# Rotary halves exchanged by transfers within SBUF instead of products on TensorE

## The chip, the cores and the metric

The kernel runs on one core of one Trainium2 chip. The metric is the device time of one execution in microseconds (us). The kernel before takes 1118.47 us, the median of three runs (1117.57 to 1119.99).

## The reference

Input is 256 tokens of width 1024. First comes one block with conditioning (scale, shift and gate from a vector c): a SwiGLU feed-forward, a token mixer and a second feed-forward. Then come two layers, each with retention (4 heads of 64), sliding-window attention with sinks (6 query and 2 key heads), latent attention (6 heads of 64 + 32 rotary dimensions), an output projection, a layer norm and a mixture of 16 experts. What the change touches is the rotary embedding of queries and keys: in the mixer (12 heads of 64), for retention's q and k (4 heads of 64), and for the last 32 dimensions of the latent queries and its one key.

```python
def apply_rope(t, cos, sin):
    t1, t2 = jnp.split(t, 2, axis=-1)
    return jnp.concatenate([t1 * cos - t2 * sin, t2 * cos + t1 * sin], axis=-1)
```

Written with the two halves of a head exchanged, this is t * cos + swap(t) * (-sin on the first half, +sin on the second).

## The kernel before

The kernel is written engine by engine, each with its own list of instructions in a fixed order, and semaphores between them; nothing schedules them later. Activations lie feature by token: 128 features on the partitions, 256 tokens along the row, so the two halves of a head are on different partitions. SBUF is the chip's working memory, PSUM the memory that TensorE (PE) writes.

Weights come from memory in units of up to 1 MB. SyncE (SP) issues their loads in order (`load`, L553 to L561) into a ring of six slots; a load waits until the slot's unit of six before has been read (`lo_made`). ScalarE (ACT) makes a half-precision copy `whi` (L444), VectorE (DVE) the remainder `wlo` (L469), and PE multiplies the pieces (L750). DVE does so for a unit three ahead of PE (`ahead` and `unit`), between its other tasks, in the order in which the code has them.

Mixer 1 projects the heads in six pairs of tiles (r = 0 to 5). Pair by pair: PE projects into PSUM; ACT evicts the raw projection to `qraw1` (`proj_out`); PE multiplies it by a 128x128 matrix `rot` of 0, 1 and -1 that exchanges the halves with their signs (`rot1`, L1119 to L1125, `rot_mm`); DVE does the rope in three operations (L2407: exchanged times sine, L2409: raw times cosine, L2410: the sum, `rope_out`).

Each layer has six ropes: r=0 the latent key (32 rows), r=1 and 2 retention's q and k, r=3 to 5 the latent queries in three pairs of heads, each with a rotation on PE in bank 7 (`rot2`, L1240 to L1247). Two more products on PE (L1383, L1384) exchange the two key heads of the sliding-window attention, `sk`, and ACT evicts the result (L2050, `swap_out`), for `scores(0)` on PE needs both orders. PE's order in this part is: projections of retention's q and k, UQ (latent queries), UKV, retention's v and gate, with `scores(p)`, `turn(p)` (transposes) and `values(p)` of six pairs of attention heads, and `ret_scores`, in between. `scores(3)` waits for `ret_d`, the four decayed products of DVE (`decayed`, L2667). DVE's order is: ropes, low parts, maxima (L2623), normalisation, copies of transposes (L2656), decays.

Of the kernel before, what the change touches and what calls it, by code (L numbers as in the profile page):

```python
# [85 lines left out]
C_IDENT, C_ROT, C_ROTM, C_ONES, C_INVF, C_EPS, C_EPSLN, C_PRIO16, C_PRIO4 = 0, 128, 256, 384, 512, 513, 514, 516, 532  # L86
# [10 lines left out]
def constants():  # L97
# [3 lines left out]
    for b in (0, 64):  # L101
        for i in range(32):
            small[b + 32 + i, C_ROT + b + i] = -1.0
            small[b + i, C_ROT + b + 32 + i] = 1.0
    for i in range(16):
        small[80 + i, C_ROTM + 64 + i] = -1.0
        small[64 + i, C_ROTM + 80 + i] = 1.0
# [27 lines left out]
    cosr, sinr = np.cos(ang64), np.sin(ang64)  # L135
    ang32 = (t[None, :].astype(np.float32) * np.tile(inv32, 2)[:, None]).astype(np.float32)
    cosm, sinm = np.ones((P, T), np.float32), np.zeros((P, T), np.float32)
    cosm[64:96], sinm[64:96] = np.cos(ang32), np.sin(ang32)
# [36 lines left out]
def build(nc, a, out):  # L175
    small_d, b1_d, b2_d = a["const_small"], a["const_block1"], a["const_block2"]
    with ExitStack() as ctx:
# [37 lines left out]
        rot = small[:, C_ROT:C_ROT + P]  # L215
# [42 lines left out]
        qraw1 = [rt1[:, 512 * i:512 * i + 512] for i in range(2)]  # L258
        rtmp1 = [rt1[:, 1024 + 512 * i:1536 + 512 * i] for i in range(2)]
# [30 lines left out]
        qraw2 = [rt2[:, 512 * i:512 * i + 512] for i in range(2)]  # L290
        rtmp2 = [rt2[:, 1024 + 512 * i:1536 + 512 * i] for i in range(2)]
# [74 lines left out]
        proj_out, rot_mm, rope_out = sem("proj_out"), sem("rot_mm"), sem("rope_out")  # L366
# [5 lines left out]
        swap_mm, swap_out, gn_in = sem("swap_mm"), sem("swap_out"), sem("gn_in")  # L372
# [177 lines left out]

        block = ctx.enter_context(nc.Block())
# [3 lines left out]
        def _(sp):  # L555
# [46 lines left out]
            for l in range(LAYERS):  # L602
                for i in range(N_LMIX):
                    load(Unit(U_L + N_L * l + i), sources[U_L + N_L * l + i])
                units, wholes = moe_units(l)
# [7 lines left out]
                for i, src in enumerate(units):  # L613
# [131 lines left out]
        def _(pe):  # L745
# [375 lines left out]
            def rot1(r):  # L1121
                pe.wait_ge(proj_out, 1 + r + 1)
                if r >= 2:
                    pe.wait_ge(rope_out, r - 1)
                pe.matmul(ps[:, 4 + r % 2, :], rot, qraw1[r % 2], start=True, stop=True).then_inc(rot_mm, 1)  # L1125

            proj_by_tokens([(Unit(U_MIX + IN1_POS[i]), 256, i) for i in range(3)], 0, [(x_new, 4), (gt_out, 4)], used)
            for i in range(2, 10):
# [10 lines left out]
                if 2 <= i < 8:  # L1139
                    rot1(i - 2)  # L1140
# [87 lines left out]
            for l in range(LAYERS):  # L1228
# [11 lines left out]
                def rot2(r, e, rows, mat):  # L1240
                    left(e)
                    if r == 1:
                        pe.wait_ge(swap_out, l + 1)
                    elif r:
                        pe.wait_ge(rope_out, rb + r)
                    n = T if rows.start else HALF
                    pe.matmul(ps[rows, 7, 0:n], mat, qraw2[r % 2][rows, 0:n], start=True, stop=True).then_inc(rot_mm, 1)  # L1247

                def rot_mla(j):
                    rot2(3 + j, 9 + j, slice(0, 96), small[0:96, C_ROTM:C_ROTM + 96])  # L1250

                def scores(p):

                    if p == 0:
                        pe.wait_ge(mask_made, 1)
                        pe.wait_ge(swap_out, l + 1)
# [108 lines left out]
                rot2(0, 3, slice(64, 96), small[64:96, C_ROTM + 64:C_ROTM + 96])  # L1365
# [15 lines left out]
                left(5)  # L1381
                pe.wait_ge(rope_out, rb + 1)
# [13 lines left out]
                rot2(1, 7, slice(0, P), rot)  # L1396
# [5 lines left out]
                rot2(2, 8, slice(0, P), rot)  # L1402
                turn(1)
                scores(2)
                rot_mla(0)
# [9 lines left out]
                rot_mla(1)  # L1415
# [3 lines left out]
                rot_mla(2)  # L1419
# [303 lines left out]
        def _(act):  # L1723
# [81 lines left out]
            def phase(ph):  # L1805
# [74 lines left out]
            for i in range(10):  # L1880
# [9 lines left out]
                elif i < 7:  # L1890
                    r = i - 1
                    if r >= 2:
                        act.wait_ge(rope_out, r - 1)
                    dst = qraw1[r % 2]
# [67 lines left out]
            for l in range(LAYERS):  # L1962
# [43 lines left out]
                def mla_query(j):  # L2006
# [4 lines left out]
                    act.wait_ge(rope_out, rb + 2 + j)  # L2011
                    leave(9 + j, qraw2[(3 + j) % 2][0:96, :], ps[0:96, j % 2, :])
# [20 lines left out]
                leave(3, qraw2[0][64:96, 0:T], ps[64:96, 5, 0:T])  # L2033
# [15 lines left out]
                act.wait_ge(swap_mm, l + 1)  # L2049
                act.activation(sk[:, 1, :], ps[:, 7, 0:T], ACT.Copy).then_inc(swap_out, 1)  # L2050
# [9 lines left out]
                leave(7, qraw2[1], ps[:, 0, :])  # L2060
# [4 lines left out]
                act.wait_ge(rope_out, rb + 1)  # L2065
                leave(8, qraw2[0], ps[:, 1, :])
# [914 lines left out]
```

## Time and profile before

| | |
|---|---|
| median of three runs | 1118.47 us |
| the profiled execution, time | 1117.76 us |
| the profiled execution, span | 1116.0 us |
| PE busy | 1077.0 us (97%) |
| DVE busy | 874.7 us (78%) |
| ACT busy | 633.1 us (57%) |
| granted TensorE clock | 0.99 |

The span is the time from the first to the last recorded instruction; the execution takes 1.8 us more. A start time in the views is counted from the span's start. Mixer 1's rotations lie between 244 and 279 us, those of the first layer between 589 and 640, those of the second between 861 and 913. Busy shares are averages; what a stretch waits for stands in the chain of waits and in the idle time before an instruction.

### The profile page before, as it was taken

The page shows a single profiled execution, that of the slowest core. Times are in us where ns is not written, and L with a number is a line of the kernel's source. Part 1 is how long each engine was busy: PE and PEld are TensorE (multiplying, and loading weights), DVE is VectorE, ACT ScalarE, POOL GpSimd, SP SyncE. Part 2 cuts the span into 40 slices and gives each one's busy share as a digit, 9 for nine tenths or more (in the row PEclk, how much of TensorE's full clock was granted, in tenths as well). Part 3 has the DMA queues.
Part 4 walks back from the last instruction along what each step waited for, and adds up shares of the span by engine and source line. Part 5 has one row for each costly group of instructions (what it writes and reads, how often), then busy time and mean ns, then how long its engine had stood idle before and what let it go on. Part 6 is the DMA issues. An engine that isn't in the chain of part 4 may idle for free.

```text
span 1116.0 us, 24969 instructions
## 1 busy us (share of the span) xinstructions
PE 1077.0 (97%) x10736; PEld 819.0 (73%) x10736; DVE 874.7 (78%) x1130; ACT 633.1 (57%) x792; POOL 90.5 (8%) x104
## 2 busy tenths in 40 slices
PE   6999999999999999999999999999999999999996
PEld 5677777688788577777778785877758877597773
DVE  4789699788787885554667967999966886799994
ACT  1544344463466554444367555877755755687771
POOL 1114621043000110000000000000000000000000
PEclk9899999999999999999999999999999999999998
DMA  9999799754556578554546226499993523579981
GB/s 340 370 371 373 278 316 359 247 177 160 189 187 229 195 254 305 194 184 167 175 143 237 94 77 231 184 378 416 414 315 107 183 89 108 222 263 396 416 363 39
DMA packets 134717, 271.94 MB, mean 244 GB/s; under 512 B 9428, under 2 KB 98104, under 8 KB 126296
## 3 DMA queue, kind: packets, MB, share of 16 engines
q1 hardware_dynamic: 124248, 231.79, 58.1%
q0 software_dynamic: 7904, 29.25, 7.3%
q10 hardware_dynamic: 2464, 9.44, 2.2%
q8 instruction: 77, 1.26, 0.5%
q14 instruction: 24, 0.20, 0.0%
HBM read 269.41 MB, written 1.05 MB: 242 GB/s over the span
## 4 chain that ended last, share of the span: by engine, by line
PE 81%; DVE 10%; ACT 4%; DMA 3%; issue 2%; ACTq 0%; DVEq 0%; SPq 0%
PE ps L750 67%; PE ps L1625 3%; DVE wlo L469 3%; DMA area<-in_w_ada_dram 2%; PE ps L1673 1%; PE ps L892 1%; PE ps L902 1%; DVE area L2841 1%; PE ps L910 1%; PE ps L1278 1%; PE ps L1247 1%; PE ps L1087 1%; DVE bnst L2282 1%; ACT area L1776 1%; PE ps L1308 1%
## 5 line engine op out<-in xcount | busy, mean ns | idle before, releaser
L469 DVE SCALAR_TENSOR_TENSOR wlo<-raw,whi 128x2048 f16<-128x2048 f32 (+4 forms) x212 | 466.0, 2231 | 36.6 <-ACT whi L444 36.0
L444 ACT ACTIVATE whi<-raw 128x2048 f16<-128x2048 f32 (+4 forms) x212 | 385.2, 1850 | 25.8 <-DMA raw<-in_w_ffn_in_dram 10.2
L750 PE MATMUL ps<-uhi,whi 128*128 128x256 f16 (+2 forms) x1328 | 329.6, 260 | 2.2 <-DVE ulo L2308 2.0
L750 PE MATMUL ps<-uhi,wlo 128*128 128x256 f16 (+2 forms) x1328 | 329.4, 260 | 0.0
L750 PE MATMUL ps<-ulo,whi 128*128 128x256 f16 (+2 forms) x1328 | 329.4, 260 | 0.0
L750 PE MATMUL ps<-whi,hreg 128*128 128x512 f16 (+1 forms) x656 | 205.0, 381 | 0.0
L750 PE MATMUL ps<-area,whi 128*128 128x96 f16 (+2 forms) x2168 | 155.0, 210 | 0.0
L750 PEld LDWEIGHTS ps<-area,whi 128*128 128x128 f16 (+2 forms) x2168 | 145.4, 99 | 11.7 <-issue 5.6
L750 PE MATMUL ps<-area,wlo 128*128 128x96 f16 (+2 forms) x1084 | 149.4, 210 | 0.0
L750 PEld LDWEIGHTS ps<-uhi,whi 128*128 128x128 f16 (+1 forms) x1328 | 130.3, 98 | 23.5 <-issue 8.9
L750 PEld LDWEIGHTS ps<-ulo,whi 128*128 128x128 f16 (+1 forms) x1328 | 130.2, 98 | 15.6 <-issue 1.9
L750 PEld LDWEIGHTS ps<-uhi,wlo 128*128 128x128 f16 (+1 forms) x1328 | 130.1, 98 | 11.5
L750 PE MATMUL ps<-wlo,hreg 128*128 128x512 f16 (+1 forms) x328 | 124.9, 381 | 0.0
L750 PEld LDWEIGHTS ps<-whi,hreg 128*128 128x128 f16 (+1 forms) x656 | 68.9, 105 | 70.6 <-issue 3.0
L750 PEld LDWEIGHTS ps<-area,wlo 128*128 128x128 f16 (+2 forms) x1084 | 107.3, 99 | 0.0
L2359 DVE SCALAR_TENSOR_TENSOR area<-area,cond 128x512 f32 (+1 forms) x94 | 72.0, 766 | 10.7 <-DMA area<-in_w_ada_dram 7.5
L1796 ACT ACTIVATE hreg<-ps 128x512 f32<-128x512 f32 x22 | 13.2, 599 | 117.1 <-PE ps L750 117.1
L750 PEld LDWEIGHTS ps<-wlo,hreg 128*128 128x128 f16 (+1 forms) x328 | 34.5, 105 | 33.5 <-issue 2.1
L2325 DVE SCALAR_TENSOR_TENSOR hreg<-ps,hreg 128x512 f32<-128x512 f32 x22 | 15.1, 688 | 46.2 <-ACT hreg L1796 46.2
L549 POOL DMA_DIRECT2D area<-in_w_ada_dram x48 | 35.0, 729 | 161.8 <-DVE area L2359 129.6
L1798 ACT ACTIVATE hreg<-hreg 128x512 f16<-128x512 f32 x22 | 13.9, 632 | 56.2 <-DVE hreg L2325 56.2
L750 PE MATMUL ps<-whi,uhi 128*128 128x256 f16 (+2 forms) x176 | 38.8, 244 | 2.0 <-DVE ulo L2310 2.0
(358 smaller groups left out, 1324.6 us busy)
## 6 DMA issues: line engine op xcount, KB each, us to landing
raw<-in_exp_w_gate_up_dram SPq DMA_DIRECT2D x64, 1024.0 KB, 8.4
raw<-in_w_ffn_in_dram SPq DMA_DIRECT2D x44, 1024.0 KB, 7.5
raw<-in_w_in_dram SPq DMA_DIRECT2D x34, 1024.0 KB, 7.0
area<-in_w_ada_dram POOLq DMA_DIRECT2D x48, 512.0 KB, 7.1
raw<-in_w_ffn_out_dram SPq DMA_DIRECT2D x22, 1024.0 KB, 7.6
raw<-in_exp_w_down_dram SPq DMA_DIRECT2D x22, 1024.0 KB, 9.2
raw<-in_w_out_dram SPq DMA_DIRECT2D x12, 1024.0 KB, 4.9
x<-in_exp_w_down_dram SPq DMA_DIRECT2D x6, 1024.0 KB, 10.1
```

The source lines that it names most:

```text
L444: act.activation(whi[:, u.slot, 0:n], raw[:, u.slot, 0:n], ACT.Copy, scale=SW)\
L469: dve.scalar_tensor_tensor(out=wlo[:, u.slot, 0:n], in0=raw[:, u.slot, 0:n], scalar=SW, in1=whi[:, u.slot, 0:n], op0=ALU.mult, op1=ALU.sub ...
L549: eng.dma_start(aring[:, j, :, :], w_ada[:, 2 * j:2 * j + 2, c0:c0 + ADA_BLOCK]).then_inc(ada_late[j], 16)
L750: last = pe.matmul(o, st, mv, start=start and i == 0, stop=stop and i == 2, skip_group_check=True)
L892: ins = pe.transpose(ps[:, 4 + 2 * t + k // 4, (k % 4) * P:(k % 4 + 1) * P], xn[:, t, k * P:(k + 1) * P], ident)
L902: pe.matmul(ps[:, bank, :], ident16, zeros16[:, :], start=True, stop=True)
L910: pe.matmul(o, st[:, k, xs], res_one, start=k % 4 == 0 and i == 0, stop=False, skip_group_check=True)
L1625: last = pe.matmul(ps[0:SLOTS, 6 + n, :], e_whole[i % 4][:, f * SLOTS:(f + 1) * SLOTS], whole[i % 2][:, f * D + n * HALF:f * D + (n + 1) * ...
L1796: act.activation(s_act, ps[:, 4 + 2 * par, :], ACT.Silu, scale=1.0 / S).then_inc(silu_made, 1)
L1798: act.activation(hhi[:, par, :], h_f32, ACT.Copy).then_inc(h_hi, 1)
L2325: dve.scalar_tensor_tensor(out=h_f32, in0=ps[:, 5 + 2 * par, :], scalar=SX / S, in1=s_act, op0=ALU.mult, op1=ALU.mult).then_inc(h_made, 1)
L2359: ins = dve.scalar_tensor_tensor(out=v, in0=w, scalar=cond[:, k:k + 1], in1=v, op0=ALU.mult, op1=ALU.add)
```

## The change

ACT now evicts a projection straight to the place where the rotated tile is to stand. SP issues transfers from SBUF to SBUF (`swap_halves`) that copy each half to the other half's partitions of a second tile `swp`; DVE multiplies that by the sine, the tile in place by the cosine, and adds. The signs of the rotation matrix stand in the sine tables (for the mixer by a column `sign` as the scale of ACT's sine). All rotation products and the two exchange products leave PE, and ACT no longer evicts the exchanged `sk`. The latent ropes work on the 32 rotary rows only. In the mixer a swap is four transfers of 32 rows of 2 KB; in a layer it is two transfers of 16 rows (latent key, and each pair of latent queries), two of 64 rows (`sk`) or four of 32 rows (retention): 24 in the mixer and 18 in a layer, 60 in all. Each swap waits for the landing of the swap before it.

```diff
+            def swap_halves(landed, halves, src, dst):
+                if landed > 32 * len(halves):
+                    sp.wait_ge(swap_in, landed - 32 * len(halves))
+                for a0, b0, n in halves:
+                    sp.dma_start(dst[a0:a0 + n], src[b0:b0 + n]).then_inc(swap_in, 16)
+                    sp.dma_start(dst[b0:b0 + n], src[a0:a0 + n]).then_inc(swap_in, 16)
+
             for i in range(N_MIX):
                 load(Unit(U_MIX + i), sources[U_MIX + i])
+                r = i - 10
+                if 0 <= r < 6:
+                    sp.wait_ge(proj_out, r + 2)
+                    if r >= 4:
+                        sp.wait_ge(rope_out, r - 3)
+                    swap_halves(mix_swapped(r), HEADS64, mix_rope_dst(r), two_tiles(swp1[r % 4]))
...
                 for i in range(N_LMIX):
                     load(Unit(U_L + N_L * l + i), sources[U_L + N_L * l + i])
+                    if i == 12:
+                        swap_key()
+                    elif i == 13:
+                        swap_sk()
+                    elif i == 16:
+                        swap_ret(1)
+                    elif i == 17:
+                        swap_ret(2)
+                        swap_mla(0)
...
                     load(Unit(U_L + N_L * l + N_LMIX + i), src)
+                    if i < 2:
+                        swap_mla(1 + i)
...
-                pe.matmul(ps[:, 4 + r % 2, :], rot, qraw1[r % 2], start=True, stop=True).then_inc(rot_mm, 1)
...
-                    pe.matmul(ps[rows, 7, 0:n], mat, qraw2[r % 2][rows, 0:n], start=True, stop=True).then_inc(rot_mm, 1)
...
-                pe.matmul(ps[0:64, 7, 0:T], ident[:, 64:128], sk[:, 0, :], start=True, stop=True)
-                pe.matmul(ps[64:128, 7, 0:T], ident[:, 0:64], sk[:, 0, :], start=True, stop=True).then_inc(swap_mm, 1)
...
-                        act.activation(sinb[:, :], tr[0], ACT.Sin)
+                        act.activation(sinb[:, :], tr[0], ACT.Sin, scale=sign)
...
-                    dst = qraw1[r % 2]
+                    act.activation(mix_rope_dst(i - 1), two_tiles(ps[:, i % 4, :]), ACT.Copy, scale=1.0 / S).then_inc(proj_out, 1)
...
-                act.wait_ge(swap_mm, l + 1)
-                act.activation(sk[:, 1, :], ps[:, 7, 0:T], ACT.Copy).then_inc(swap_out, 1)
...
+            def rope(made, landed, rows, cos, sin, swapped, dst, k):
+                dve.wait_ge(swap_in, landed)
                 cb, sbc = (v[rows, :].unsqueeze(1).to_broadcast([rows.stop - rows.start, k, T]) for v in (cos, sin))
+                sw, d = swapped[rows, 0:k * T].rearrange("p (k n) -> p k n", k=k), dst[rows]
+                dve.tensor_tensor(sw, sw, sbc, ALU.mult).then_inc(dve_step, 1)
                 n_step[0] += 1
+                link(dve.tensor_tensor(d, d, cb, ALU.mult))
+                dve.tensor_tensor(d, sw, d, ALU.add).then_inc(rope_out, 1)
```

How SP's order changes in a layer, from the load of the unit UKV to the first expert weights (`raw` is the ring, `area` and `xn` hold activations, in brackets the semaphores that an instruction waits for). Before:

```order
L561 DMA raw<-in_mla_w_ukv_dram 128x2x768 [waits lo_made]
L561 DMA raw<-in_w_in_dram 128x8x256 [waits lo_made] x2
L561 DMA raw<-in_w_out_dram 128x2x1024 [waits lo_made] x4
L561 DMA raw<-in_router_w_dram 128x8x16 [waits lo_made]
L561 DMA raw<-in_exp_w_gate_up_dram 128x2048 [waits lo_made] x4
```

And the same place of SP's order in the changed kernel, up to the swap of retention's k:

```order
L588 DMA raw<-in_mla_w_ukv_dram 128x2x768 [waits lo_made]
L588 DMA raw<-in_w_in_dram 128x8x256 [waits lo_made] x2
L630 DMA area<-xn 16x256 [waits swap_in,rope_out,proj_out]
L631 DMA area<-xn 16x256
L588 DMA raw<-in_w_out_dram 128x2x1024 [waits lo_made]
L630 DMA area<-area 64x256 [waits swap_in,proj_out]
L631 DMA area<-area 64x256
L588 DMA raw<-in_w_out_dram 128x2x1024 [waits lo_made] x3
L630 DMA area<-area 32x512 [waits swap_in,proj_out]
...
L588 DMA raw<-in_router_w_dram 128x8x16 [waits lo_made]
L630 DMA area<-area 32x512 [waits swap_in,proj_out]
```

The key's swap stands behind the second of the two loads of `w_in`, that of retention's q behind the last load of `w_out`, that of retention's k behind the router's; a load that follows a swap is now issued after the swap's waits.

DVE around the first rope of mixer 1, before:

```order
L469 SCALAR_TENSOR_TENSOR wlo<-raw,whi 128x2048 [waits hi_made] x2
L2407 TENSOR_TENSOR area<-ps,sinb 128x512 [waits rot_mm]
L2409 TENSOR_TENSOR area<-area,cosb 128x512
L2410 TENSOR_TENSOR area<-area 128x512 [waits dve_step]
L469 SCALAR_TENSOR_TENSOR wlo<-raw,whi 128x2048 [waits hi_made,rope_out]
```

And the same instructions of DVE in the changed kernel:

```order
L463 SCALAR_TENSOR_TENSOR wlo<-raw,whi 128x2048 [waits hi_made] x2
L2440 TENSOR_TENSOR area<-area,sinb 128x512 [waits swap_in]
L2442 TENSOR_TENSOR area<-area,cosb 128x512
L2443 TENSOR_TENSOR area<-area 128x512 [waits dve_step]
L463 SCALAR_TENSOR_TENSOR wlo<-raw,whi 128x2048 [waits hi_made,rope_out]
```

DVE keeps its place and number of instructions; what moved is its wait, from a product on PE (`rot_mm`) to a transfer's landing (`swap_in`), and the next low part still stands behind it.

## Rows read from the trace of the kernel before

**Rows 1.** The page, busy time, share of the span and instructions of each engine.

```profile
PE 1077.0 (97%) x10736; PEld 819.0 (73%) x10736; DVE 874.7 (78%) x1130; ACT 633.1 (57%) x792; POOL 90.5 (8%) x104
```

**Rows 2.** Busy time by stretch: us, PE, PEld, DVE, ACT, POOL, PEclk, DMA, GB/s.

```profile
244.00:292.40 48.40, 48.18 (x408) 39.29 (x404) 41.71 (x48) 20.13 (x19) 17.76 (x17) 1.00 0.70 230
589.00:643.00 54.00, 53.64 (x449) 41.91 (x447) 45.94 (x82) 33.62 (x66) 0.00 (x0) 1.00 0.47 157
```

**Rows 3.** Chain of waits of mixer 1: start us, us, what.

```profile
251.11 0.86 PE ps L1125 x2
...
292.34 0.49 PE ps L1004 x4
```

**Rows 4.** Chain of waits of the first layer.

```profile
589.35 0.54 PE ps L1247 x2
...
621.80 0.69 DVE area L2407
...
623.96 1.07 PE ps L1247 x2
...
641.29 0.33 PE ps L1274 x2
```

**Rows 5.** Instructions of line 1247: duration ns min/median/max, first and last start, forms.

```profile
L1247 PE MATMUL ps<-area,small x24: 374/592/670, 589.3 to 911.9; 96*96 96x512 f32 x12, 128*128 128x512 f32 x8, 32*32 32x256 f32 x4
```

**Rows 6.** Instructions of lines 2407 and 2409 in mixer 1, on DVE.

```profile
L2407 DVE TENSOR_TENSOR area<-ps,sinb x6: 678/688/693, 247.1 to 280.2; 128x512 f32<-128x512 f32 x6
...
L2409 DVE TENSOR_TENSOR area<-area,cosb x6: 675/681/764, 247.7 to 280.8; 128x512 f32<-128x512 f32 x6
```

**Rows 7.** Timeline of SP's queue: start us, us to the last one's end, line.

```profile
244.50 0.37 SPq L561 DMA_DIRECT2D raw<-in_w_ada_dram  x1
...
587.62 1.50 SPq L561 DMA_DIRECT2D raw<-in_w_in_dram  x2
...
620.16 0.37 SPq L561 DMA_DIRECT2D raw<-in_router_w_dram  x1
632.36 21.62 SPq L561 DMA_DIRECT2D raw<-in_exp_w_gate_up_dram  x4
```

**Rows 8.** DMA issues at 244.6, 588.8, 610.7, 674.4, 674.9, 1111: us to landing last.

```profile
raw<-in_w_ada_dram SPq DMA_DIRECT2D x1, 1024.0 KB, 5.6
...
raw<-in_w_in_dram SPq DMA_DIRECT2D x1, 1024.0 KB, 7.3
...
raw<-in_w_out_dram SPq DMA_DIRECT2D x1, 1024.0 KB, 4.8
...
x<-in_exp_w_down_dram SPq DMA_DIRECT2D x1, 1024.0 KB, 7.5
...
gt<-in_exp_w_down_dram SPq DMA_DIRECT2D x1, 1024.0 KB, 9.6
...
out_dram<-x SPq DMA_DIRECT2D x4, 256.0 KB, 2.1
```

**Rows 9.** Timeline of DVE: start us, us, instruction, in brackets idle time before.

```profile
247.13 0.68 DVE L2407 TENSOR_TENSOR area<-ps,sinb 128x512 f32<-128x512 f32 x1
...
589.93 0.42 DVE L2407 TENSOR_TENSOR area<-ps,area 32x256 f32<-32x256 f32 x1 [1.21 <-PE ps L1247]
...
595.33 1.75 DVE L2683 RECIPROCAL area<-area 128x256 f32<-128x256 f32 x1 [1.86 <-ACT area L2039]
...
607.22 0.62 DVE L2623 TENSOR_REDUCE x<-ps 128x1 f32<-128x128 f32 x2 [0.71 <-PE ps L1278]
...
608.80 1.75 DVE L469 SCALAR_TENSOR_TENSOR wlo<-raw,whi 128x1536 f16<-128x1536 f32 x1
...
615.80 0.68 DVE L2407 TENSOR_TENSOR area<-ps,area 128x512 f32<-128x512 f32 x1
...
636.51 0.68 DVE L2407 TENSOR_TENSOR area<-ps,area 96x512 f32<-96x512 f32 x1
```

**Rows 10.** Waits of mixer 1: engine, line, waited for, us in total, times, longest.

```profile
DVE area L2407 <- PE ps L1125: 3.2, 3, 1.8
```

More of the change, by code:

```diff
@@ L100, in constants @@
     small[:, C_IDENT:C_IDENT + P] = np.eye(P)
[L101 to L107, printed above, removed]
+    sign64 = np.where(np.arange(P) % 64 < 32, -1.0, 1.0).astype(np.float32)
+    sign32 = np.where(np.arange(32) < 16, -1.0, 1.0).astype(np.float32)
+    small[:, C_SIGN] = sign64
     small[:, C_ONES:C_ONES + P] = 1.0
@@ L214, in build @@
         ident = small[:, C_IDENT:C_IDENT + P]
-        rot = small[:, C_ROT:C_ROT + P]
+        sign = small[:, C_SIGN:C_SIGN + 1]
         ones = small[:, C_ONES:C_ONES + P]
@@ L257, in build @@
         pt1 = [v[:, 0:1152].rearrange("p (g n) -> p g n", g=3) for v in (rt1, merged)]
-        qraw1 = [rt1[:, 512 * i:512 * i + 512] for i in range(2)]
-        rtmp1 = [rt1[:, 1024 + 512 * i:1536 + 512 * i] for i in range(2)]
+        swp1 = [rt1[:, 512 * i:512 * i + 512] for i in range(4)]
         gtmp = [sb1[0].rearrange("p g n -> p (g n)")[:, 0:512], sb1[0].rearrange("p g n -> p (g n)")[:, 512:1024],
@@ L289, in build @@
         rt2 = tk(2048)
-        qraw2 = [rt2[:, 512 * i:512 * i + 512] for i in range(2)]
-        rtmp2 = [rt2[:, 1024 + 512 * i:1536 + 512 * i] for i in range(2)]
+        swp2 = [rt2[:, 512 * i:512 * i + 512] for i in range(4)]
         masks16 = tk(384, dt=BF16).rearrange("p (i n) -> p i n", i=2)
@@ L549, in ada_block, with swaps_landed, mix_swapped, layer_swapped @@
                 eng.dma_start(aring[:, j, :, :], w_ada[:, 2 * j:2 * j + 2, c0:c0 + ADA_BLOCK]).then_inc(ada_late[j], 16)
+        HEADS64, HALF32, KV_HEADS = ((0, 32, 32), (64, 96, 32)), ((64, 80, 16),), ((0, 64, 64),)
+        S_KEY, S_SK, S_RETQ, S_RETK, S_MLA = 0, 1, 2, 3, 4
+        MIX_SWAPS, LAYER_SWAPS = (HEADS64,) * 6, (HALF32, KV_HEADS, HEADS64, HEADS64, HALF32, HALF32, HALF32)
+        def swaps_landed(n):
+            order = MIX_SWAPS + LAYER_SWAPS * LAYERS
+            return sum(32 * len(order[i]) for i in range(n))
+        def mix_swapped(r):
+            return swaps_landed(r + 1)
+        def layer_swapped(l, i):
+            return swaps_landed(len(MIX_SWAPS) + len(LAYER_SWAPS) * l + i + 1)
+        def mix_rope_dst(r):
+            return (q1, k1)[r // 3][:, 2 * (r % 3):2 * (r % 3) + 2, :]
+        def ret_rope_dst(r):
+            return rqk[:, 2 * (r - 1):2 * (r - 1) + 2, :]
+        def mla_rope_dst(j):
+            return qm[:, 2 * j:2 * j + 2, :]
+        def two_tiles(v):
+            return v.rearrange("p (k n) -> p k n", k=2)
         block = ctx.enter_context(nc.Block())
@@ L2059, in _ @@
                 done(RET_Q)
-                leave(7, qraw2[1], ps[:, 0, :])
+                leave(7, ret_rope_dst(1), two_tiles(ps[:, 0, :]))
                 unit(RET_K)
@@ L2397, in phase @@
                 steps(dve, ph, step)
[L2399 to L2405 removed]
+            def rope(made, landed, rows, cos, sin, swapped, dst, k):
+                dve.wait_ge(swap_in, landed)
                 cb, sbc = (v[rows, :].unsqueeze(1).to_broadcast([rows.stop - rows.start, k, T]) for v in (cos, sin))
[L2407 removed]
+                sw, d = swapped[rows, 0:k * T].rearrange("p (k n) -> p k n", k=k), dst[rows]
+                dve.tensor_tensor(sw, sw, sbc, ALU.mult).then_inc(dve_step, 1)
                 n_step[0] += 1
[L2409 to L2411 removed]
+                link(dve.tensor_tensor(d, d, cb, ALU.mult))
+                dve.tensor_tensor(d, sw, d, ALU.add).then_inc(rope_out, 1)
+                dve.wait_ge(rope_out, made)
             def mix_masked(p, gs):
@@ L2606, in _ @@
                     dve.tensor_copy(masks16, masks2).then_inc(mask_made, 1)
-                full, mla, h0 = slice(0, P), slice(0, 96), 4 + 12 * l
+                full, part, h0 = slice(0, P), slice(64, 96), 4 + 12 * l
                 def unit(i):
@@ L2669, in rope_ret @@
                 def rope_ret(r):
-                    rope(r, rb, full, tables[:, 0, :], tables[:, 1, :], qraw2[r % 2], rtmp2,
-                         rqk[:, 2 * (r - 1):2 * (r - 1) + 2, :], 2, 7)
+                    rope(rb + r + 1, layer_swapped(l, (S_RETQ, S_RETK)[r - 1]), full, tables[:, 0, :], tables[:, 1, :], swp2[r],
+                         ret_rope_dst(r), 2)
                 def rope_mla(j):
-                    rope(3 + j, rb, mla, tables[:, 2, :], tables[:, 3, :], qraw2[(3 + j) % 2], rtmp2,
-                         qm[0:96, 2 * j:2 * j + 2, :], 2, 7)
+                    rope(rb + 3 + j + 1, layer_swapped(l, S_MLA + j), part, tables[:, 2, :], tables[:, 3, :], swp2[(3 + j) % 4],
+                         mla_rope_dst(j), 2)
                 for i in (LAT01, LAT2, LAT34, KEY_ROPE):
                     unit(i)
-                rope(0, rb, slice(64, 96), tables[:, 2, :], tables[:, 3, :], qraw2[0], rtmp2, kro[64:96, :].unsqueeze(1), 1, 7)
+                rope(rb + 1, layer_swapped(l, S_KEY), part, tables[:, 2, :], tables[:, 3, :], swp2[0], kro.unsqueeze(1), 1)
                 unit(SWA_Q)
```

75 lines of the change are left out of this document (27 added, 48 removed).

## The prediction

> **What bounds the kernel now.** I read the page's busy times first, then busy time by stretch, then the chain of waits, then the two stretches that the change touches engine by engine. TensorE (PE) is busy 1077.0 of 1116.0 us, VectorE (DVE) 874.7 [rows 1], so over the whole run every microsecond taken off PE looks like a gain. That average hides what counts. In the stretch of mixer 1 that holds the six rotations, PE is busy 48.18 of 48.40 us but DVE 41.71; in the stretch of a layer that holds its six rotations PE is busy 53.64 of 54.00 and DVE 45.94 [rows 2]. A DVE that is 85% busy and works in a fixed order, with PE waiting for what it makes, is the second bound, close behind the first. The chain of waits says so: in the mixer it lies on PE alone, a rotation of 0.86 us between two projections [rows 3], but in the layer it leaves PE and runs over DVE, the rope of r=2 at 621.80 in it, until it comes back at 623.96 with a rotation on PE [rows 4]. So PE can lose the rotations and gain no more than DVE, and what DVE waits for, allow.
>
> **What goes.** On PE a rotation takes 0.86 us of the chain in the mixer, six times 5.2 us [rows 3]. In a layer one takes 0.54 (the key of 32 rows) and five take about 0.86 to 1.07 [rows 4]; with 24 records for two layers [rows 5] that is 2 x (0.54 + 5 x 0.95) = 10.6 us. Some 16 us of PE work are gone; the two key-exchange products per layer add less than a rotation each. ScalarE (ACT) loses one eviction per layer, which nobody waits for long, and I count it as nothing: the same instant is now set by a transfer.
>
> **What stays.** DVE keeps its three operations per rope. The first reads SBUF now and no longer PSUM. The rows put the two side by side: 688 ns with a PSUM operand, 681 ns with both in SBUF, same shape [rows 6]. I take no change, bounds -0.1 to +0.1 us a rope. The MLA ropes shrink from 96 rows to 32, at the same 512 columns; the key rope of 32 rows by 256 columns takes 0.42 against 0.68 [rows 9], which goes with the columns, so I take nothing for rows either.
>
> **What comes.** 60 transfers within SBUF are issued by SP, and SP is the engine that issues the weight loads, in order. One issue is 0.37 us [rows 7], so four are 1.5 and all sixty 22 us over the run; SP has that time. What counts is when a swap lands. Its place in SP's list is just behind a 1 MB load, and DVE's rope now waits for the landing. No swap is in the trace of before, so its price needs bounds. The nearest small transfers are the four output stores of 256 KB at the end, 2.1 us from issue to landing with nothing ahead of them [rows 8]. For two transfers behind each other there is a row too: two 1 MB loads issued within 0.8 us land 7.5 and 9.6 us after their issue, one after the other and not side by side [rows 8]. A swap behind a load should so land when the load has landed and its own 64 KB have passed. At 1 MB in about 2 us of spacing, 64 KB is a sixteenth: 0.13 us each, 0.3 us for two and 0.5 for four. Lower end: with the load (+0). Upper end: the load's landing and then the whole 2.1 us. I take 0.3 to 0.5, since the spacing of the two loads is the nearest row, and 2.1 after the last issue where the load ahead is small.
>
> **Mixer 1, step by step.** Swap 0 stands behind the load issued at 244.50, which lands 5.6 us after its issue, 250.1 [rows 7, 8]; the rope begins at 250.5 and not at 247.13 [rows 9]: DVE stands 3.4 us. What it gains back is its waits for PE's rotations, 3.2 us in three ropes [rows 10]; by the same working swaps 2 and 4 cost about 1 us each, since they too stand behind a load of 5 us or more, and the others land in time. DVE so ends this stretch about where it did, 0.7 us later, and PE, relieved of 5.2 us, waits for the low parts that DVE makes (two idle microseconds before projection 9). The attention scores that begin at 292.34 on PE [rows 3] begin about 1.2 us earlier, as the tail on PE and ACT is shorter: -1.2 us rather than -5.2.
>
> **A layer, step by step (times of layer 0).** (1) The key swap stands behind the second of the two loads at 587.62, issued at 588.8, which takes 7.3 us [rows 7, 8]: 596.1, swap 596.3, and the rope was at 589.93 [rows 9]. DVE is 6.4 us late. Its idle times of 1.86 before the reciprocal at 595.33 and of 0.71 before the maxima at 607.22 [rows 9] swallow 2.6; 3.8 stay. (2) The low part at 608.80, 1.75 long [rows 9], now ends at 614.3 and releases the load that was issued at 610.7 and landed 4.8 us later [rows 8]. It lands at 619.2, the swap for retention's q at 619.5; its rope was at 615.80 [rows 9]: +3.7, so just the lateness that is there. (3) The next low part releases the router's load at 623.8 (620.16 before [rows 7]); the swap for retention's k stands behind it, its four issues end at 625.4, and with 2.1 us it lands at 627.5. Its rope was at 621.80 [rows 4]: +5.7. (4) DVE goes on from there through two copies, maxima, one MLA rope and a low part; about half a microsecond of idle is swallowed there (an estimate, as the idle times of rows 9), and the expert load that was issued at 632.36 [rows 7] goes at 637.4, lands 5.2 us later (an estimate: as the 4.8 and 5.6 of rows 8), and the swap of MLA pair 1 behind it at 642.9. DVE, 5 us late, arrives at that rope (636.51 before [rows 9]) at 641.5 and stands 1.4 us more. The rope's 2.05 us and the two decayed products behind it end at 645.9, and the scores of pair 3 that PE began at 641.29 [rows 4] begin at about 646.1: +4.9 us. What is behind DVE's rope in its order is the low parts and decays that PE needs, so the wait reaches PE whole. From there PE has projections to do that need nothing of this, and the last MLA swap hides behind them.
>
> **Sum.** 2 x 4.9 - 1.2 = +8.6 us. The profiled execution took 1117.76 us, so 1126.4; the median of the runs is 0.7 above it, so 1127. With the swaps at the lower end (landing with their loads) the layers' steps shrink by 0.3 to 0.5 each and the sum is about +5.3: 1124. At the upper end each swap behind a big load comes 1.8 us later still: two or three of them decide in the mixer (+5) and two or three in each layer (+4.5 each), about +22.6: 1141. The likeliest case's own range is 1123 to 1136.
>
> **Rivals.** *Swaps that do not queue (faster).* Place: the swaps behind 1 MB loads. If a swap passes the load and lands 2.1 us after its last issue, the key swap lands at 592 and is swallowed by the idle times, retention's q and MLA pair 1 are in time, and only retention's k is late, 2.3 us instead of 5.7, since it still stands behind a low part that DVE must make first. Then the layers gain 0.7 each and the mixer 4.1: -5.5, 1113. It decides where a swap lands within about 3 us of its issue although a load is in flight. For it: transfers are spread over 16 engines, and a load does not fill them at every instant (DMA share 0.47 in the layer [rows 2]). Against it: the two loads that land in order. The Trainium skill, in "DMA: Bandwidth & Descriptors", section "Queues, rings and completion order", says both things: on each DMA engine descriptors are consumed in ring order, yet completion is not FIFO per issuing engine. By the first half the sum is the forecast's, by the second this rival's; the two loads of rows 8 land in the order of their issue and so speak for the first. *Dearer swaps.* A transfer that reads and writes SBUF in pieces of 1 or 2 KB could cost more than a sixteenth of a load, or each swap wait its full 2.1 us since it waits for the one before: +16 to +23, 1134 to 1141. For it: the swaps of one kind are chained, and SP issues none before the last has landed; against it: 64 KB is little. *Nothing changes.* The 4.9 us of a layer are made up later, at the router or where PE waits for weights, and the 16 us less of PE work pays it: within 2 us of before. Against it: PE is busy over 99% of the stretch [rows 2] and the work behind it is PE's own. *The full gain.* DVE's waits vanish as the rotations do and PE's 16 us come off: 1102. It needs every swap to land before its rope's old start, which the key swap, issued 1 us before that start, cannot.
>
> **How the numbers follow.** A difference below 0.2% (2.2 us) is what a measurement of this kernel cannot tell from none. Forecast 0.66, dearer swaps 0.12, nothing changes 0.09, no queueing 0.11, full gain 0.02. Slower is 0.66 + 0.12 = 0.78, same 0.09, faster 0.13. The range goes from the faster rival's upper edge, 1115, to 1138, which leaves out the top of the dear case and the best of the fast one. Predicted: 1127 us.
>
> **What would show it.** In the profile after: no rotation rows on PE; DVE rows of the rope's first line with idle times put down to a transfer, about 3 us once in the mixer and 6, 0 to 1, 2 and 1 to 2 us for the key, q, k and MLA pair 1 of each layer; swap transfers of 16 to 64 rows that land 5 to 8 us after their issue behind a load and about 2 us elsewhere; new PE idle time of some 10 us a layer (the 4.9 and the rotations' 5.3), put down to DVE; DVE's busy time unchanged. Swaps that land 2 to 3 us after issue everywhere, or PE idle time that did not grow by 15 us over the run, would make me wrong.

## The result: 1143.95 us, 2.4% slower

The changed kernel takes 1143.95 us (median of four runs, 1141.52 to 1145.40) against 1118.02 beside it: the ratio is 1.0238, 95% interval 1.0218 to 1.0258. The profiled execution spans 1143.5 us against 1116.0, 27.5 more. The forecast was 1127 us, with a range up to 1138. The direction was right; the loss is three times the forecast.

The page's busy times and two stretches of the profile after, cut at the same work as [rows 2] (columns as there):

```profile
PE 1074.5 (94%) x10692; PEld 819.2 (72%) x10692; DVE 874.5 (76%) x1130; ACT 631.9 (55%) x790; POOL 90.2 (8%) x104
```

```profile
244.00:297.20 53.20, 46.34 (x399) 39.11 (x396) 41.73 (x48) 20.32 (x19) 17.96 (x17) 0.94 0.74 231
594.00:659.60 65.60, 55.17 (x435) 43.14 (x434) 45.59 (x80) 33.11 (x65) 0.00 (x0) 0.90 0.44 142
```

DVE has nearly the same work as before in both stretches (41.73 and 45.59 us) and they last 4.8 and 11.6 us longer: it stands. PE lost some 16 us of rotations and yet is busy only 2.5 us less [rows 1]: what is left ran slower, since the granted clock is 0.94 and 0.90 here where it was 1.00.

Where DVE stands is in its timeline of mixer 1 and the first layer (start, us, instruction, idle time before it and what ended it):

```profile
251.65 0.69 DVE L2440 TENSOR_TENSOR area<-area,sinb 128x512 f32<-128x512 f32 x1 [4.07 <-DMA area<-area]
...
264.79 0.69 DVE L2440 TENSOR_TENSOR area<-area,sinb 128x512 f32<-128x512 f32 x1 [2.39 <-DMA area<-area]
...
278.12 0.69 DVE L2440 TENSOR_TENSOR area<-area,sinb 128x512 f32<-128x512 f32 x1 [3.03 <-DMA area<-area]
...
602.31 0.42 DVE L2440 TENSOR_TENSOR area<-area 32x256 f32<-32x256 f32 x1 [8.74 <-DMA area<-xn]
...
616.85 0.62 DVE L2655 TENSOR_REDUCE x<-ps 128x1 f32<-128x128 f32 x2
...
626.43 0.69 DVE L2440 TENSOR_TENSOR area<-area 128x512 f32<-128x512 f32 x1 [0.71 <-DMA area<-area]
...
635.96 0.69 DVE L2440 TENSOR_TENSOR area<-area 128x512 f32<-128x512 f32 x1 [3.52 <-DMA area<-area]
...
652.53 0.68 DVE L2440 TENSOR_TENSOR area<-area 32x512 f32<-32x512 f32 x1 [2.43 <-DMA area<-area]
```

These are ropes of mixer 1 and of [rows 4, 9], and at 616.85 the first maxima; the idle time before each rope is put down to a swap's landing. Held against the starts before, they show how the lateness grows. Mixer 1 leaves 4.84 us: its scores begin at 297.18 and not at 292.34 [rows 3]. On top of that, in the first layer, the key rope is 7.5 late, the first maxima 4.8, retention's q 5.8, its k 9.3, MLA pair 1 11.2, and scores 3 on PE (655.65 for 641.29 [rows 4]) 9.5. A low part that DVE makes before the second layer's ropes closes the sum (before, then after):

```profile
854.54 2.29 DVE L469 SCALAR_TENSOR_TENSOR wlo<-raw,whi 128x2048 f16<-128x2048 f32 x1 [4.56 <-ACT whi L444]
```

```profile
870.98 2.29 DVE L463 SCALAR_TENSOR_TENSOR wlo<-raw,whi 128x2048 f16<-128x2048 f32 x1 [4.56 <-ACT whi L438]
```

It is 16.44 us late, so the first layer loses 11.6; the span's 27.5 leaves 11.1 for the second.

The chain of waits of the first layer has the swaps in it, which is what the forecast meant, and between them the low parts that release the loads (here the one at 618.52 and the load at 620.20):

```profile
594.99 7.29 DMA area<-xn
...
618.52 1.67 DVE wlo L463
...
620.20 0.37 SPq L588
...
622.53 3.88 DMA area<-area
...
633.13 2.81 DMA area<-area
...
646.87 5.64 DMA area<-area
...
655.65 0.50 PE ps L1327 x2
```

And what it did to PE, in three stretches of idle time and the work behind each (columns as in [rows 2]):

```profile
280.60:284.20 3.60, 0.00 (x0) 0.00 (x0) 3.38 (x8) 2.39 (x2) 0.00 (x0) 1.00 0.16 39
284.20:291.00 6.80, 5.58 (x26) 4.19 (x27) 6.73 (x6) 0.00 (x0) 0.00 (x0) 0.50 0.88 282
609.60:613.00 3.40, 0.00 (x0) 0.03 (x1) 3.37 (x4) 1.64 (x3) 0.00 (x0) 0.84 0.35 125
613.00:618.50 5.50, 5.50 (x26) 3.31 (x27) 5.43 (x11) 2.78 (x6) 0.00 (x0) 0.50 0.67 232
651.90:655.60 3.70, 0.13 (x1) 0.00 (x0) 2.99 (x5) 0.49 (x1) 0.00 (x0) 1.00 0.58 218
655.60:659.60 4.00, 3.95 (x17) 2.98 (x18) 1.93 (x3) 0.00 (x0) 0.00 (x0) 0.59 0.02 9
```

```profile
656.30:659.60 3.30, 3.30 (x14) 2.39 (x13) 1.93 (x3) 0.00 (x0) 0.00 (x0) 0.50 0.02 6
...
632.40:635.80 3.40, 3.40 (x17) 2.03 (x16) 0.04 (x1) 0.49 (x1) 0.00 (x0) 0.50 0.41 88
```

Each time PE stands for 3.4 to 3.7 us, work behind it runs at a granted clock of 0.50 (1.2 of 2.4 GHz). The 0.59 is a mean: the stretch begins at the full clock, and from 656.30 on it is 0.50 too. Behind a shorter stand of 1.8 us, from 629.9 to 631.7, the clock was 0.50 as well, from 632.4 to 635.8. The idle time is paid once by waiting and a second time by slow products.

### The profile page after: what moved, and what is told of

Same layout as the page of the kernel before. It is cut to its first block, busy times and chain, and to the rows that moved or that the text cites. A ratio compares the mean times of both kernels' runs of the same rounds, so it can differ in the third digit from the quotient of the medians.

```text
span 1143.5 us, 24930 instructions
## 1 busy us (share of the span) xinstructions
PE 1074.5 (94%) x10692; PEld 819.2 (72%) x10692; DVE 874.5 (76%) x1130; ACT 631.9 (55%) x790; POOL 90.2 (8%) x104
## 4 chain that ended last, share of the span: by engine, by line
PE 67%; DVE 16%; DMA 7%; ACT 4%; issue 3%; SPq 2%; ACTq 0%; DVEq 0%
PE ps L823 56%; DVE wlo L463 5%; DMA area<-area 3%; PE ps L1667 3%; DMA area<-in_w_ada_dram 2%; DMA area<-xn 1%; SPq L630 1%; PE ps L1715 1%; PE ps L965 1%; PE ps L975 1%; ACT whi L438 1%; DVE area L2440 1%; DVE area L2443 1%; DVE area L2873 1%; PE ps L983 1%
## 5 line engine op out<-in xcount | busy, mean ns | idle before, releaser
L2395 DVE SCALAR_TENSOR_TENSOR area<-area,cond 128x512 f32 (+1 forms) x94 | 72.0, 766 | 11.1 <-DMA area<-in_w_ada_dram 7.9
```

What stands on the lines that cost most here:

```text
L2395: ins = dve.scalar_tensor_tensor(out=v, in0=w, scalar=cond[:, k:k + 1], in1=v, op0=ALU.mult, op1=ALU.add)
```

## The experiments

Theories: **place** (the price is the swap's place behind a 1 MB load, which DVE and then PE wait out), **price** (transfers from SBUF to SBUF are dear in themselves, on any queue), **clock** (PE's idle time costs most, by the clock behind it). Each ratio below is to the kernel before, measured beside that kernel, with its 95% interval. In all kernels below the ropes take the tile in place and the signs from the tables, as after; where products exchange the halves, their matrix has no signs.

### Mixer 1 alone, the layers alone

```diff
-mixer 1: rot1 on PE                      +mixer 1: swap_halves on SP     (e1_mixer)
-layers: rot2, exchange of sk on PE       +layers: swap_halves on SP      (e2_layers)
```

> Swaps in mixer 1 only; in the layers TensorE's products exchange the halves, as before. Matching DVE's instructions of the two traces one by one, the changed kernel is 4.8 us late when mixer 1 ends. If the losses of the parts simply add, this kernel takes 4 to 6 us more than before, 1122 to 1124. If the layers' swaps and the mixer's hang together, or the lateness is made up when the layers have their products again, it is within 2 us of before.

> Swaps in the two layers only; mixer 1 has its products on TensorE. Adding theory: 11.7 and 11.0 us for the two layers, so 1139 to 1143. Rival: the mixer's lateness made the layers worse, then less than 1135.

Measured: 1.0048 (1.0030 to 1.0066) and 1.0186 (1.0156 to 1.0217). The layers alone take 1137.1 us, a little less than the 1139 to 1143 expected. The parts add to 1.0234, the whole is 1.0238: within the intervals, neither makes the other worse.

### The layers' swaps on GpSimd's queue

```diff
-swap_layer(sp, ...)  behind the loads
+swap_layer(pool, ...)  # all seven of a layer, as soon as the eviction is done
```

> As the kernel with swaps in the layers only, but the layers' swaps are issued by GpSimd on its own queue, where no weight load stands ahead of them and SP's loads don't wait behind them. Queue theory (the price is the place behind 1 MB loads and SP's issues): the key's swap lands 3 to 4 us after its issue instead of 7, each layer loses 0 to 4 us instead of 11, 1118 to 1126. Price theory (a transfer from SBUF to SBUF is dear in itself, or shares the 16 engines with the loads in flight on any queue): landing stays at 5 us and more, 1134 to 1143.

Measured: 1.0037 (1.0026 to 1.0048), from 1.0186. Some 16 of 21 us are gone, so most of the price is the place in SP's order. But the landing times fit neither theory. Issues at 586.9 and at 629.9 in that run, kind, number, size, us to landing:

```profile
area<-xn POOLq DMA_DIRECT2D x2, 16.0 KB, 4.9
...
area<-area POOLq DMA_DIRECT2D x2, 32.0 KB, 1.7
```

The key's swap, 16 KB a piece, alone on its queue, takes 4.9 us in the median of its two pieces; one of twice the size takes 1.7. The first was issued 0.4 us after a 1 MB load on SP's queue, the second when none was in flight. The rope shows the same:

```profile
592.42 0.42 DVE L2560 TENSOR_TENSOR area<-area 32x256 f32<-32x256 f32 x1 [4.86 <-DMA area<-xn]
```

So a queue of its own did not take this swap past the load in flight; what it can save is that the swap is issued before the next load, and that SP's loads do not wait for it. The Trainium skill states a rule that bears on this in "DMA: Bandwidth & Descriptors", section "Issuing engines are not separate DMA queues": transfers of any issuing engine run on the same 16 DMA engines and interleave, and several issuers save only the time to issue. The 4.9 us are in keeping with it; the 16 us come from the order of issue, of which it does not speak.

### The same with the loads held back

```diff
 for i in range(N_LMIX):
+    if i == 11: sp.wait_ge(swap_in, layer_swapped(l, S_KEY))
+    if i == 16: sp.wait_ge(swap_in, layer_swapped(l, S_RETQ))
     load(...)
```

> All layer swaps issued by GpSimd, mixer 1 with products; and SP holds back the loads 11 and 16 of each layer until the key's swap and that of retention's q have landed, so that no load is in flight beside these two. In the run without the hold they landed 4.5 to 5.0 us after issue, with a load in flight, and 1.7 to 2.0 where none was. Contention theory (a swap lands with the load in flight, whatever queue it is on): 1.7 to 2.3 us for both now, DVE's waits of 4.9 and 3.1 us fall to 2 and 0 to 1, and the kernel comes from 1.0037 to 0.998 to 1.001. Rival (these swaps are dear because of their shape or the first use of a queue): landing stays above 4 us. Either way the held loads could come late and TensorE wait for low parts: then it stays above 1.003 with short landings.

Measured: 0.9930 (0.9909 to 0.9951). The key's swap at 587.9 and the whole run's swaps of that kind:

```profile
area<-xn POOLq DMA_DIRECT2D x2, 16.0 KB, 2.0
...
area<-xn POOLq DMA_DIRECT2D x4, 16.0 KB, 2.0
```

Same queue, same shape, same place in the program; what is gone is the load issued just ahead of it (an earlier load, due to land 0.8 us later, was still in flight), and 4.9 us become 2.0. The kernel is faster than the 0.998 to 1.001 expected, and faster than before.

### SP's queue again, swap ahead of the load

```diff
 for i in range(N_LMIX):
+    if i == 11: swap_layer(sp, 'sp', l, S_KEY)
+    elif i == 14: swap_layer(sp, 'sp', l, S_SK)
+    elif i == 16: swap_layer(sp, 'sp', l, S_RETQ)
+    elif i == 17: swap_layer(sp, 'sp', l, S_RETK); swap_layer(sp, 'sp', l, S_MLA)
     load(Unit(U_L + N_L * l + i), sources[U_L + N_L * l + i])
-    if i == 12: ...   # the same swaps behind loads 12, 13, 16, 17
```

The diff is shortened. The key's swap so moves ahead of two loads (11 and 12); that of the key heads keeps its place between loads 13 and 14; the last two latent pairs move ahead of the first two expert loads, so the very last still stands behind one of them.

> The changed layers with all swaps on SP's queue again, mixer 1 with products, and one thing moved in SP's order: a swap stands ahead of the load that it stood behind (key ahead of load 11, key heads ahead of 14, retention's q ahead of 16, its k and the first latent pair ahead of 17, the other two pairs ahead of the first two expert loads). To be held against the layers' swaps behind the loads, 1.0186. Order theory (the price was the load ahead or in flight, not SP's queue): swaps land 2 to 3 us after issue, 0.993 to 0.999, near the run on GpSimd's queue with held loads, 0.993. Queue theory (SP's queue and its issues of 0.59 us are dear in themselves, or the loads that now wait for swaps come late): above 1.005.

Measured: 0.9932 (0.9909 to 0.9955), where the same swaps behind the loads gave 1.0186. The whole run's swaps by kind, first behind the loads, then ahead of them:

```profile
area<-area SPq DMA_DIRECT2D x20, 64.0 KB, 4.0
area<-area SPq DMA_DIRECT2D x12, 32.0 KB, 2.8
area<-xn SPq DMA_DIRECT2D x4, 16.0 KB, 6.5
```

```profile
area<-area SPq DMA_DIRECT2D x20, 64.0 KB, 2.0
area<-area SPq DMA_DIRECT2D x12, 32.0 KB, 2.0
area<-xn SPq DMA_DIRECT2D x4, 16.0 KB, 2.9
```

The number of transfers, their shapes, their queue and DVE's order are the same. A few lines of SP's order are worth 2.5% of the kernel. The rope of the first layer's key waits 2.56 us, no longer than the transfer itself takes:

```profile
590.48 0.42 DVE L2563 TENSOR_TENSOR area<-area 32x256 f32<-32x256 f32 x1 [2.56 <-DMA area<-xn]
```

### Mixer 1: another queue, another order

> Swaps in mixer 1 only, issued by ScalarE on its own queue right behind its eviction; in the layers products on TensorE. To be held against the run with SP's swaps in mixer 1 only, which took 0.48% more than before. Place theory: behind no load and issued earlier, the swaps land before DVE wants them, -2 to +1 us against before. Contention theory: a swap shares the DMA engines with the load in flight and lands with it on any queue: +3 to +6 us.

Measured on ScalarE's queue: 1.0040 (1.0027 to 1.0052), against 1.0048 on SP's: no gain clear of noise, and in the range of the contention theory. The swaps landed no sooner (4.2 us in the median, 3.8 on SP's queue), and a new wait came. In the waits of that run, 244 to 300 us, the engine and line that waits, for what, us in all, times, longest:

```profile
ACT whi L452 <- DMA area<-area: 7.1, 2, 3.7
...
DVE wlo L477 <- ACT whi L452: 8.5, 3, 3.5
```

Before it issues a swap, ScalarE waits for the landing of the swap before, and the conversion of the weights stands behind that. So this run doesn't tell the queue from the new wait; the next one keeps SP's queue.

> Swaps on SP's queue in mixer 1 only, each ahead of the load that it stood behind; layers with products. Behind the loads this was 1.0048 of before, on ScalarE's queue 1.0040. If the mixer's price has the same cause as the layers' (the load ahead or in flight), the swaps land 2 to 3 us after issue and the kernel is 0.995 to 1.000. If the mixer differs, because loads are nearly always in flight there (DMA share 0.7) or because loads held behind a swap come late for DVE and TensorE: 1.002 or more.

The edit is the layers' in mixer 1: `swap_mix(sp, 'sp', r)` ahead of `load(Unit(U_MIX + i), ...)`. Measured: 0.9977 (0.9960 to 0.9994), a gain where it was a loss of 0.48%. DVE's waits for swaps in mixer 1 (us in all, times, longest), first behind the loads, then ahead of them:

```profile
DVE area L2560 <- DMA area<-area: 9.1, 3, 4.5
```

```profile
DVE area L2563 <- DMA area<-area: 0.9, 1, 0.9
```

The price in mixer 1 was the place in SP's order too. But the swaps did not land 2 to 3 us after their issue, as expected, since earlier loads are still in flight there: a piece takes 3.0 us in the median, 3.8 behind the loads. The first swap is issued 1.9 us sooner (241.5 for 243.4) and is complete 3.4 us sooner (246.9 for 250.2).

### The clock

```diff
+                warm('sc0')     # 16 products of zeros into an unused PSUM bank
                 scores(0)
```

This is one of seven such places, three in mixer 1 and four in a layer.

> The changed kernel, with products of zeros (128x512, about 0.21 us each at the full clock) put into TensorE's order where it stood idle longest: 8, 16 and 6 in mixer 1, and 16, 8, 5 and 16 before scores 0, turn 1, values 1 and scores 3 of each layer. They do nothing but keep TensorE busy while it waits. Clock theory (TensorE's idle time costs twice, since the granted clock falls to half behind it, and that is most of the 26 us): 10 us or more come back, 1134 or less. DVE theory (TensorE waits for DVE anyway, the half clock matters only behind scores 3 and at the mixer's end): 3 to 6 us come back, 1138 to 1141. Nothing: the clock is an effect and no cause, 1142 to 1146.

Measured: 1.0190 (1.0165 to 1.0216) from 1.0238, so about 5.4 us, and the mean granted clock is 0.991 instead of 0.978 (0.990 before). The fillers before scores 0 of the first layer in that run's timeline of PE (start, us, instruction), and the stretch of 5.5 us from scores 0 on:

```profile
605.37 3.62 PE L1010 MATMUL ps<-zeros,diag 128*128 128x512 f16 x16
```

```profile
608.80:614.30 5.50, 5.50 (x50) 4.40 (x49) 5.43 (x10) 2.81 (x9) 0.00 (x0) 1.00 0.82 291
```

The idle time is filled, the clock stays at 1.00, and 50 products fit where 26 did. Yet only about a fifth of the loss comes back, though the mean clock is that of the kernel before: PE waits for DVE and DVE for swaps whatever the clock. The clock makes the loss larger; it is not its cause.

### No exchange at all

> No rotation products and no swaps: DVE's rope takes the tile itself where the exchanged one should stand (the exchange of halves is left out; only the key heads of the window attention are still exchanged on TensorE). It shows what there is to win. If DVE is the second bound, as the prediction had it, PE's 16 us come off only in part: 1106 to 1114. If PE alone bounds, 1101 to 1104. If TensorE then idles and its clock falls, the gain is eaten: 1112 to 1120.

Measured: 0.9914 (0.9889 to 0.9939), 9.6 us of PE's 16. The stretch of mixer 1 in that run (columns as in [rows 2]), and the stand of PE at its end, with what ended it:

```profile
242.52:287.20 44.68, 42.98 (x396) 37.30 (x393) 43.11 (x48) 20.22 (x19) 18.72 (x17) 1.00 0.71 232
```

```profile
287.14 0.49 PE L1112 MATMUL ps<-area 64*128 64x128 f32 x4 [1.70 <-DVE hreg L2683]
```

DVE is now as busy as PE (43.11 and 42.98 of 44.68 us), and PE waits for it; in the first layer PE stands twice, 1.0 and 1.2 us, and for DVE both times, and so it does in the second. These stands make 6.2 us, close to the 6.4 that are missing. So with no transfer in the way the rest of the 16 us is lost to DVE, and the prediction's first step (PE can gain no more than DVE allows) stands.

### Exchange by ScalarE's evictions

```diff
+def act_halves(dst, src):   # PSUM to SBUF, 32 rows each, to the other half's partitions
+    for a0, b0, n in HEADS64:
+        act.activation(dst[a0:a0 + n, :], src[b0:b0 + n, :], ACT.Copy, scale=1.0 / S)
+        act.activation(dst[b0:b0 + n, :], src[a0:a0 + n, :], ACT.Copy, scale=1.0 / S)
```

> Mixer 1 without products and without transfers: ScalarE evicts each tile four more times, 32 rows each, with the halves exchanged, since it may write other partitions than it reads; layers with products as before. If the exchange is made by an engine with time to spare, the mixer's share of the gain that the run without any exchange showed (5.2 us late in the mixer by DVE's instructions) comes: 3 to 6 us faster than before. If ScalarE becomes the bound (four evictions of about 0.6 us, 14 us more in the mixer): slower by 1 to 5 us.

> As the run before it, and in the layers ScalarE writes the exchanged halves of retention's q and k and of the key heads too; the latent key and queries (halves of 16 rows) keep their products on TensorE. If it adds up: 6 to 9 us faster than the kernel before. If ScalarE is late with the exponentials in the layers: no faster than the run with mixer 1 alone.

Measured: 0.9973 (0.9960 to 0.9986) with mixer 1 alone, 2.9 us and so just short of the 3 to 6 expected; with retention and the key heads too 0.9995 (0.9980 to 1.0009), no gain at all. In the layers ScalarE has the exponentials of the attention to make; in the second run PE stands before the transposes of pair 1, which wait for DVE's normalisation of these exponentials:

```profile
617.67 1.01 PE L1417 MATMUL ps<-small,xn 128*128 128x128 f32 x6 [2.23 <-DVE xn L2801]
```

In the run with mixer 1 alone PE does not stand at that place:

```profile
619.35 0.82 PE L1417 MATMUL ps<-small,xn 128*128 128x128 f32 x6
```

That ScalarE's four extra evictions per tile (0.59 us each) delay the exponentials is read from this, not tested by itself.

### Together

> Mixer 1 with ScalarE's exchanged evictions (that run alone: 0.9973 of before), in the layers only the latent queries' three swaps by transfers that GpSimd issues; these are issued where no load is in flight and landed 1.7 to 2.4 us after issue in the run with all layer swaps on GpSimd. If a swap costs nothing where nothing is in flight and DVE comes later anyway, the three rotations of about 0.9 us per layer come off as well: 0.992 to 0.995. If DVE is the bound there: 0.997, as without them. If the swaps still make DVE stand: above 0.998.

> As the run before it, with ScalarE's exchanged evictions in mixer 1: no rotation product is left on TensorE. If the parts add: 0.003 less than the run before it, 0.995 to 0.998.

> Layers' swaps on SP's queue ahead of the loads (0.9932 with products in mixer 1), and ScalarE's exchanged evictions in mixer 1 (0.9973 alone). If the parts add: 0.989 to 0.992. If DVE or ScalarE bounds both: 0.993 and no better than one alone.

Measured: 0.9942 (0.9922 to 0.9961), 0.9922 (0.9904 to 0.9941) and 0.9917 (0.9888 to 0.9945; 1107.71 us). In the first, DVE waits for none of the swaps, which are issued with no load in flight, and three of them per layer bring 0.3%. The last two stand within noise of the run without any exchange, 0.9914. Whether the parts add is not shown: mixer 1's gain, 0.0027 alone, shows as 0.0008 and 0.0015 on top of the layers', neither clear of the intervals. The second kernel, expected at 0.995 to 0.998, was better than that because the kernel with held loads already was.

## Why the prediction was wrong, point by point

**DVE as the second bound: right.** PE lost 16 us and the kernel could not win more than 9.6.

**A swap lands with the load ahead of it: right, and the cause.** The key's load, 8.4 us long from 593.6, lands at 602.0, its swap at 602.28: 0.3 us, as forecast. The sizes were off elsewhere. The last of four pieces lands 0.9 us after its load (626.41, the load at 625.5), not 0.5; with two pieces MLA pair 1's does too (652.51, the load at 651.6). The working put 64 KB at a sixteenth of 2 us, but its two loads land 2.5 us apart (issued 0.4 us apart, then 7.5 and 9.6 us [rows 8]), by which four pieces take 0.6 us. And the issues are dearer. All issues of the second line of the swap, ns, shortest, median, longest:

```profile
L631 SPq DMA_DIRECT2D area<-area x28: 581/592/2482, 246.7 to 936.7; - x28
```

The prediction took 0.37 us, the issue of a load [rows 7]. At 0.59 and up to 2.5 us, four issues take 2.4 us and more; in mixer 1 the first swap's four run from 245.29 to 248.87, and the last of them lands at 251.63 and not at 250.5.

**Mixer 1, "DVE so ends this stretch about where it did": this step failed.** DVE stood 4.1, 2.4 and 3.0 us (9.5) for swaps 0, 2 and 4, where 3.4, 1 and 1 were worked out, and in place of a gain of 1.2 us there was a loss of 4.8. Of these 6 us, 4.1 are the longer waits. Another 1.5 are a slip in the sum: 3.4, 1 and 1 less the 3.2 gained back leave DVE 2.2 us late, not 0.7. (Measured, it is 6.1 us late at the low part that began at 282.22 before and begins at 288.34 now.) The shorter tail behind that gave back 1.3 us and not 1.9. The clock has a share in the loss: PE idles 3.6 us and does projection 9 at half the clock, and with zeros in PE's gaps the way from the low part at 242.06 before to the one at 585.30 grows by 2.9 us instead of 4.6 (by the starts of the same instructions, 240.02 and 586.16 there, 242.26 and 590.14 in the changed kernel).

**A layer: the steps right in order and place, the terms too small.** Lateness forecast and measured: key 6.4 and 7.5; first maxima 3.8 and 4.8; q 3.7 and 5.8; k 5.7 and 9.3; MLA pair 1 6.4 and 11.2; scores 3 4.9 and 9.5. Each step hands its excess to the next, as the working had it, since a low part releases the next load and that load carries the next swap. What each adds of its own is read from the loads ahead of the key, q and MLA pair 1, and from the first and last issue for k:

```profile
raw<-in_w_in_dram SPq DMA_DIRECT2D x1, 1024.0 KB, 8.4
...
raw<-in_w_out_dram SPq DMA_DIRECT2D x1, 1024.0 KB, 5.3
...
raw<-in_exp_w_gate_up_dram SPq DMA_DIRECT2D x1, 1024.0 KB, 5.8
```

```profile
631.28 0.54 SPq L630 DMA_DIRECT2D area<-area  x1
...
633.13 1.42 SPq L631 DMA_DIRECT2D area<-area  x1
```

The loads themselves took 1.1, 0.5 and 0.6 us longer than the 7.3, 4.8 and 5.2 of the working; the last pieces of q and of MLA pair 1 came 0.6 us later each; and the four issues for k took 3.3 us instead of 1.5, of which 1.5 reach the rope. Together that is, within 0.1, the 4.8 us by which MLA pair 1 is later than forecast. From scores 3 to the second layer the loss grows from 9.5 to 11.6 us, where the working ended its sum.

**What the sum left out.** TensorE's clock: the prediction let PE idle ten more microseconds a layer and priced the products behind at full clock; filling the gaps with zeros brings back 5.4 of the 26 us. Behind scores 3 the 3.4 us at 0.50 would be 1.7 us of the growth to 11.6, an estimate from the rows of the stretch above. The wait of scores 0 for the key heads' swap: it made PE stand from 609.6 to 613.0 and was not in the working; DVE came to the maxima at 616.85 without waiting for these scores, so the stand itself cost little. The clock behind it made the next scores late: DVE's next maxima begin at 623.60 after an idle time of 2.09 us, about as long as before (1.86), so that none of DVE's lateness is made up there; with zeros in the gap that idle time is 0.16, and 1.7 us are made up. Sum: 21 us without the clock, close to the upper end of 22.6 that the prediction worked out for swaps that come 1.8 us later each. The range was cut below that end, with too little chance for it.

**The rival of swaps that do not queue: not borne out.** A single piece did pass a load. These are the expert load issued at 649.80, and the first and second piece of the last MLA swap, issued at 652.58 and 653.14:

```profile
raw<-in_exp_w_gate_up_dram SPq DMA_DIRECT2D x1, 1024.0 KB, 7.5
...
area<-area SPq DMA_DIRECT2D x1, 32.0 KB, 2.3
...
area<-area SPq DMA_DIRECT2D x1, 32.0 KB, 4.5
```

The first piece lands 2.5 us ahead of the load, the second 0.3 us behind it, and the rope waits for both. In all traces, on three different queues, the last piece of a swap landed at most 0.2 us ahead of a load in flight, and nearly always behind it. Put ahead of the load, the layers' swaps land after 2 to 3 us, save the last latent pair's, and those kernels are faster than before; but that is another order, and no test of the rival's price. **Dearer swaps** had the range nearest to the time (1134 to 1141). Its reason does not hold, since a piece nearly always lands within the 2.1 us of the working when no load is in flight; what was dearer is the issue.

## What to carry to other kernels

Here a small transfer issued just behind a large load cost about the load's time, and on another queue too. So put the transfer that is waited for ahead of the bulk, or hold the bulk until it has landed, before judging the idea. When work is taken off the busiest engine, look at the second one (here 85% busy and in a fixed order) and count what the first engine's new idle time does to its clock. And a negative result of a good idea may be one line of issue order: here 1.0186 and 0.9932.

## What the runs showed of the hardware

- A piece of a swap, 16 to 64 KB from SBUF to SBUF, landed 1.7 to 2.1 us after its issue when no load was in flight from its issue to its landing (68 of 72 pieces in the traces of all kernels; the other four 2.3 to 3.1). Issued less than 2 us behind a 1 MB load it took 3.0 to 7.5 us, 4.8 in the median of 112, whichever of three engines issued it.
- One issue of such a transfer on SP takes 0.59 us in the median against 0.37 for a weight load, and now and then 1.4 to 2.5 us.
- TensorE's granted clock was 0.50 behind each idle time of 3.4 to 3.7 us in mixer 1 and the first layer, and behind one of 1.8 us. It was 1.00 throughout where products of zeros filled the gap before scores 0.
- Three operations of one rope in mixer 1, beside a GpSimd busy 5.69 of 6.00 us, took 1.20, 1.21 and 1.09 us instead of 0.68. The two are seen together; that one causes the other was not tested. DVE's busy time in the stretch is the same as before (41.73 and 41.71 us).
